# First two column chunks of five stages computed token-major, with the first token tile's part ahead of the second tile's norm

## The reference, cut to what matters

```
h  = norm1(h)                              RMS norm over the 1024 features
cols = h @ w_in                            34 chunks of 256 columns: gates, q, k, v, ...
     recurrence on the first chunks, attention, branches, output product
h  = h + mix
h  = h + (relu(norm2(h) @ w_up) ** 2) @ w_down
```

## Time and profile before

| | us |
|---|---|
| median of 3 runs | 2162.5 (2162.14 to 2163.11) |
| the profiled execution, device time | 2162.1 |
| its span in the trace | 2160.7 |
| PE busy | 2121.8 (98%) |
| DVE busy | 1542.2 (71%) |
| ACT busy | 1337.1 (62%) |
| POOL busy | 42.6 (2%) |
| granted TensorE clock, mean of the run | 0.998 of full |

### The profile page before, as it was taken

The page is one execution under the profiler, slowest core; times in us unless marked ns, Lnnn a source line. Parts: engine busy times, 40 slices in busy tenths (PEclk is TensorE's granted clock), DMA queues, the critical chain, the costliest instruction groups (busy, mean ns, idle before and its releaser), DMA issues.

```text
span 2160.7 us, 31792 instructions
## 1 busy us (share of the span) xinstructions
PE 2121.8 (98%) x13336; PEld 1907.5 (88%) x13336; DVE 1542.2 (71%) x1736; ACT 1337.1 (62%) x1580; POOL 42.6 (2%) x44
## 2 busy tenths in 40 slices
PE   6999999999999999999999899999999999999998
PEld 6899989888888888888888799998998999998986
DVE  5565565699999899989999676666554676666544
ACT  4544436588878887887878474564553654755543
POOL 0000000100000000000000000000110000000100
PEclk9999999999999999999999999999999999999999
DMA  8455554499999999999999555544655465545652
GB/s 280 136 189 186 195 173 144 127 360 361 344 354 371 332 374 349 367 342 358 367 362 372 169 181 167 172 147 142 201 202 192 159 196 170 167 138 158 193 195 78
DMA packets 301591, 511.46 MB, mean 237 GB/s; under 512 B 10496, under 2 KB 177536, under 8 KB 301440
## 3 DMA queue, kind: packets, MB, share of 16 engines
q1 hardware_dynamic: 296464, 498.63, 67.7%
q10 hardware_dynamic: 4976, 10.70, 1.5%
HBM read 503.53 MB, written 1.05 MB: 234 GB/s over the span
## 4 chain that ended last, share of the span: by engine, by line
PE 94%; DVE 5%; issue 1%; ACT 0%; DMA 0%; DVEq 0%; ACTq 0%
PE bank L390 28%; PE bank L392 28%; PE bank L391 28%; PE bank L1756 1%; PE bank L417 1%; PE bank L1352 1%; PE bank L1231 1%; DVE w_low L370 1%; PE bank L423 1%; PE bank L1289 1%; DVE h L553 1%; DVE h L549 1%; DVE stats L542 1%; PE bank L2019 0%; PE bank L1995 0%
## 5 line engine op out<-in xcount | busy, mean ns | idle before, releaser
L370 DVE TENSOR_TENSOR w_low<-raw,w_high 128x1024 fp32r<-128x1024 f32 x938 | 1135.9, 1222 | 420.9 <-ACT w_high L359 405.5
L359 ACT CAST w_high<-raw 128x1024 fp32r<-128x1024 f32 x938 | 979.8, 1052 | 452.4 <-PE bank L392 430.0
L390 PE MATMUL bank<-x,w_high 128*128 128x256 f32 x1712 | 481.6, 281 | 0.0
L391 PE MATMUL bank<-x,w_high 128*128 128x256 f32 x1712 | 477.9, 279 | 0.0
L392 PE MATMUL bank<-x,w_low 128*128 128x256 f32 x1712 | 477.5, 279 | 0.0
L390 PE MATMUL bank<-w_high,x 128*128 128x512 f32 (+1 forms) x976 | 342.9, 351 | 0.0
L392 PE MATMUL bank<-w_high,x 128*128 128x512 f32 (+1 forms) x976 | 338.6, 347 | 0.0
L391 PE MATMUL bank<-w_low,x 128*128 128x512 f32 (+1 forms) x976 | 338.4, 347 | 0.0
L390 PEld LDWEIGHTS bank<-x,w_high 128*128 128x128 f32 x1712 | 321.9, 188 | 0.4
L391 PEld LDWEIGHTS bank<-x,w_high 128*128 128x128 f32 x1712 | 321.9, 188 | 0.2
L392 PEld LDWEIGHTS bank<-x,w_low 128*128 128x128 f32 x1712 | 321.8, 188 | 0.0
(11 more groups left out here) (326 smaller groups left out, 2555.2 us busy)
## 6 DMA issues: line engine op xcount, KB each, us to landing
raw<-in_moe_wd SPq DMA_DIRECT2D x88, 1024.0 KB, 5.5
raw<-in_w_in SPq DMA_DIRECT2D x84, 1024.0 KB, 5.2
raw<-in_moe_wg SPq DMA_DIRECT2D x80, 1024.0 KB, 5.4
raw<-in_moe_wu SPq DMA_DIRECT2D x80, 1024.0 KB, 5.4
raw<-in_w_up SPq DMA_DIRECT2D x32, 1024.0 KB, 5.4
raw<-in_w_down SPq DMA_DIRECT2D x32, 1024.0 KB, 4.9
raw<-in_w_out SPq DMA_DIRECT2D x16, 1024.0 KB, 4.9
raw<-in_ffn_wg SPq DMA_DIRECT2D x11, 1024.0 KB, 5.3
```

The source lines that it names most:

```text
L359: q.copy(high, raw).then_inc(st.cast, 1)
L370: q.tensor_tensor(low, raw, high.bitcast(F32), ALU.subtract).then_inc(st.low_made, 1)
L390: T.matmul(out, stationary[0], moving[0], start=start, stop=False, skip_group_check=True)
L391: T.matmul(out, stationary[0], moving[1], start=False, stop=False, skip_group_check=True)
```

## The change

At five stage entries `tensor_transposes` and `first_product` give way to `tensor_entry`. The first two chunks (four pieces) are now computed token-major: x is stationary, 256 weight columns move, and the output has tokens on partitions. So tile 0's part needs only tile 0's x. After turning tile 0, PE runs its high x high and high x low matmuls, then turns tile 1, then does tile 0's low x high, then tile 1's part whole. The number of product matmuls stays at 96 of 256 columns. Every `used` count of the four pieces comes in the last part. The chunks are then copied (or gated, or squared) as they are, turned to feature-major by four transposes each (`tensor_turned`) after piece 4 (in the feed-forward after pieces 4 and 5, one product of the two chunks), and evicted or split from there.

On ACT and DVE, the copies of tile 0's x stand ahead of tile 1's square and scale, and the addition of tile 1 stands behind tile 0's scale. The casts of the new stage's pieces 1 to 3 stand ahead of these copies. The low halves of pieces 1 to 3 (at layer 0's entry, of piece 3 alone) go from DVE to POOL (`gpsimd_lows`). Matmuls on constants are fewer: 4 and 1 for 8, 2 and 2 in four entries of this kind, 15 and 1 for 26, 1 and 2 at layer 0. The mixers' entries stay.

```diff
+def tensor_entry(k, src, ready, spin_bank, spins, banks):
+    T, st, base = k.nc.tensor, k.weights, 4 * k.transposed
+    first = st.next_piece
+    st.next_piece += 4
+    weights = [st.views(first + i)[1:] for i in range(4)]
+    def part(c, half, t, x_half, w_half):
+        out, w = tile2(k.banks[banks[c]])[:, t, :], weights[2 * c + half][w_half]
+        for kk in range(KT // 2):
+            i = half * (KT // 2) + kk
+            mm = T.matmul(out, k.x[x_half][:, i, t * P:(t + 1) * P], w[:, kk, :],
...
+    tensor_spin(k, spin_bank, spins[0])
+    tensor_turn(k, src, ready, 0)
+    tensor_spin(k, spin_bank, spins[1])
+    for half in range(2):
+        T.wait_ge(k.sem("x_high_made"), base + half + 1)
+        for c in range(2):
+            T.wait_ge(st.cast, first + 2 * c + half + 1)
+            part(c, half, 0, 0, 0)
+    for piece in range(4):
+        if piece == 3:
+            tensor_spin(k, spin_bank, spins[2])
+            tensor_turn(k, src, ready, 1)
+            for half in range(2):
+                T.wait_ge(k.sem("x_made"), base + half + 1)
+                for c in range(2):
+                    part(c, half, 0, 1, 0)
+        T.wait_ge(st.low_made, first + piece + 1)
+        part(*divmod(piece, 2), 0, 0, 1)
+    for c in range(2):
+        for half in range(2):
+            T.wait_ge(k.sem("x_high_made"), base + half + 3)
+            part(c, half, 1, 0, 0)
+            part(c, half, 1, 0, 1)
+        for half in range(2):
+            T.wait_ge(k.sem("x_made"), base + half + 3)
+            part(c, half, 1, 1, 0).then_inc(k.used, 1)
+def gpsimd_lows(k, upto):
+    q, st = k.nc.gpsimd, k.weights
+    while st.next_low <= upto:
+        raw, high, low = st.views(st.next_low)
+        q.wait_ge(st.cast, st.next_low + 1)
+        q.wait_ge(st.low_made, st.next_low)
+        q.tensor_tensor(low, raw, high.bitcast(F32), ALU.subtract).then_inc(st.low_made, 1)
...
 def tensor_layer(k, a, layer):
...
-    for n in range(N_COLS):
+    tensor_entry(k, a.xn, [rms_ready(k, t) for t in range(TT)], 3, (4 if layer else 15, 1, 0), LAYER_ENTRY)
+    for n in range(2, N_COLS):
         for half in range(2):
             tensor_columns(k, layer, n, half)
+            if (n, half) == (2, 0):
+                for c in range(2):
+                    T.wait_ge(k.sem("entered"), 2 * layer + c + 1)
+                    tensor_turned(k, entered(a, c), k.banks[LAYER_TURNED[c]]).then_inc(k.sem("entry_turned"), 1)
...
 def scalar_layer(k, a, layer):
...
-        if p % 2 and p < AT_BRANCH:
+        if p == 4:
+            for c in range(2):
+                scalar_evict(k, a, layer, c)
         scalar_recurrence(k, a, layer, p)
         sides.at(p)
+        if p in (1, 3):
+            scalar_entry(k, a, layer, p // 2)
+        elif p % 2 and p < AT_BRANCH:
             scalar_evict(k, a, layer, p // 2)
...
 def scalar_mlp(k, m, layer):
...
-    for t in range(TT):
-        scalar_rms(k, t, m.xn[:, t, :], norm_source(k, t))
+    scalar_rms(k, 0, m.xn[:, 0, :], norm_source(k, 0))
     scalar_casts(k, k.weights, base + PAIRS - 1)
-    scalar_transposes(k)
+    scalar_transposes(k, (0,))
+    scalar_rms(k, 1, m.xn[:, 1, :], norm_source(k, 1))
+    scalar_transposes(k, (1,))
...
 def vector_mlp(k, m, layer):
...
+    vector_rms(k, 0, m.xn[:, 0, :], *gains)
+    vector_add(k, SUMS, 1, (k.used, base))
+    vector_transposes(k, (0,))
+    vector_rms(k, 1, m.xn[:, 1, :], *gains)
+    vector_transposes(k, (1,))
```

More of the change, by code:

```diff
@@ L461, in tensor_transposes @@
-    ident = k.shared_const("ident")
     for t in range(TT):
         tensor_spin(k, bank, spins[t])
[L464 to L469, removed]
-    tensor_spin(k, 7, spins[TT])
+        tensor_turn(k, src, ready, t)
+    tensor_spin(k, 7, spins[TT])
@@ L551, in vector_layer_norm, with vector_scale @@
     own.up()
+def vector_scale(k, t):
+    V, h, gains = k.nc.vector, k.h, k.gains
+    st, mv, rstd, var = norm_columns(k, t)
     vector_root(k, var, rstd)
@@ L908, in tensor_ffn @@
                     T.wait_ge(k.sem("gate_out" if which == 0 else "gated"), j - 1)
[L909 to L912, removed]
+                mm = product(k, piece, k.x, half, 2 * (j % 2) + which, False)
                 mm.then_inc(k.used, 1)
+            if j == 1 and which == 0:
+                T.wait_ge(k.sem("gated"), 1)
+                tensor_turned(k, m.gate[0], k.banks[4]).then_inc(k.sem("entry_turned"), 1)
     for i in range(FT - TAIL):
@@ L2118, in tensor_columns, with entered, scalar_entry @@
     tokens = n in (VH, VH + 1) or VA <= n < AB
-    mm = product(k, piece, k.x, half, bank_of(n), tokens) if n else first_product(k, piece, half, 0)
-    mm.then_inc(k.used, 1)
+    product(k, piece, k.x, half, bank_of(n), tokens).then_inc(k.used, 1)
+LAYER_ENTRY, LAYER_TURNED = (4, 5), (6, 7)
+def entered(a, c):
+    return a.g[:, 2 * c:2 * c + 2, :]
+def scalar_entry(k, a, layer, c):
+    A_ = k.nc.scalar
+    A_.wait_ge(k.used, AT_LAYER[layer] + 2 * c + 2)
+    A_.copy(entered(a, c), tile2(k.banks[LAYER_ENTRY[c]])).then_inc(k.sem("entered"), 1)
 def tensor_branch(k, src, layer, u, ready):
@@ L2245, in vector_layer @@
     sides = attention_sides(lambda w: vector_attention(k, a, layer, w))
-    for t in range(TT):
-        vector_rms(k, t, a.xn[:, t, :], k.norm1, (k.sem("loaded_norm1"), 16 * (layer + 1)))
-    vector_transposes(k)
+    gains = k.norm1, (k.sem("loaded_norm1"), 16 * (layer + 1))
+    vector_rms(k, 0, a.xn[:, 0, :], *gains)
+    if layer == 0:
+        vector_scale(k, 1)
+    else:
+        vector_add(k, SUMS, 1, (k.used, base))
+    vector_transposes(k, (0,))
+    vector_rms(k, 1, a.xn[:, 1, :], *gains)
+    vector_transposes(k, (1,))
     for p in range(AT_OUT + KT - TAIL):
@@ L2282, in tensor_mlp @@
                 T.wait_ge(k.sem("relu"), 16 * layer + j - 3)
-            mm = product(k, piece, k.x, half, j % 4, False) if j else first_product(k, piece, half, 0)
-            mm.then_inc(k.used, 1)
+            product(k, piece, k.x, half, j % 4, False).then_inc(k.used, 1)
+            if (j, half) == (2, 0):
+                for c in range(2):
+                    T.wait_ge(k.sem("squared_up"), 16 * layer + c + 1)
+                    tensor_turned(k, m.relu[c], k.banks[MLP_TURNED[c]]).then_inc(k.sem("entry_turned"), 1)
     for i in range(NT2 - TAIL):
@@ L2319, in vector_mlp @@
     V, base = k.nc.vector, AT_LAYER[layer] + AT_UP
-    for t in range(TT):
-        vector_rms(k, t, m.xn[:, t, :], k.gains[:, 1, :], (k.sem("loaded_norm2"), 16 * (layer + 1)))
-    vector_transposes(k)
-    vector_lows(k, k.weights, base + PAIRS - 1)
+    gains = k.gains[:, 1, :], (k.sem("loaded_norm2"), 16 * (layer + 1))
+    vector_rms(k, 0, m.xn[:, 0, :], *gains)
+    vector_add(k, SUMS, 1, (k.used, base))
+    vector_transposes(k, (0,))
+    vector_rms(k, 1, m.xn[:, 1, :], *gains)
+    vector_transposes(k, (1,))
     for j in range(NT2 // 2):
@@ L2334, in vector_mlp @@
     vector_add(k, SUMS, 0, (k.sem("half_done"), k.halves))
-    vector_add(k, SUMS, 1, (k.used, base + 2 * NT2))
+    if layer + 1 == DEPTH:
+        vector_add(k, SUMS, 1, (k.used, base + 2 * NT2))
 def gpsimd_mlp(k, m, layer):
```

140 lines of the change are left out of this document (100 added, 40 removed).

## The result

The changed kernel takes 2172.8 us (median of 5, 2171.8 to 2173.2), the kernel before 2162.6 in the same rounds: ratio 1.0046, 95% interval 1.0031 to 1.0060. It is slower by 10 us, where 10 us faster was forecast. Beside the experiments the kernel before took 2161.9 to 2162.0 us, so times of different rounds compare to about 0.6 us. The profiled execution took 2171.8 us, its span is 2170.4, the mean granted clock 0.993 of full.

The account below looks back on a forecast made before the run. PE was taken to bound the kernel (94% of the chain). Gains of 3.5 + 1.7 + 1.9 + 0.9 + 1.9 = 9.9 us off 2162.1 gave 2152.2, with 0.4 for the median 2152.6 us; range 2148.8 to 2158.0.

Parts of the forecast that it names:

- GpSimd's low halves: At the entries: GpSimd's subtractions, 2.38 to 3.16 us each, stay hidden; cost 0, bounds 0 and 1 us in four entries.
- slower: Whole kernel: the outcome of being slower by over 0.2%, given a chance of 0.04.
- the five gains: Feed-forward 3.5 us, layer 0 1.7, its MLP 1.9, layer 1 0.9, its MLP 1.9.
- Tile 1's turning: PE's transposes of tile 1 at the entries: at 119.65 in the feed-forward, 7.0 us into the MLPs.
- What the layers give back: In each layer PE waits for DVE's low halves, 0.7 us at piece 8 and 0.2 at piece 13: 0.9 back.
- Rival 1: At the layers ACT is the new bound, both give all back: 2155.2 us, 2158 with late copies; chance 0.17.
- rival 4: At the entries tile 1's norm is later by as much, only the feed-forward gains: 2159 us; chance 0.06.
- Rival 2: At four entries GpSimd is late, 4 us and more per subtraction, costing 2 us each: 2160 to 2161; chance 0.05.
- Rival 3: At the new entries each of ten pauses drops PE's clock for 5 us: 15 us slower, 2177; chance 0.04.

Follow-up runs that it names:

- e1: Changed kernel with GpSimd's subtractions cut to 2 of 256 columns per row, the rest of those low halves left out: 2151.9 us, ratio 0.9951.
- e7: Changed kernel with each of GpSimd's subtractions cut into eight of 128 columns: 2168.5 us, ratio 1.0030.
- e11: Changed kernel with each of GpSimd's subtractions cut into four of 256 columns: 2158.45 us, ratio 0.9984.
- e10: Changed kernel, GpSimd's low halves starting only after tile 1's scale, PE first taking what needs no new low half, constants refitted: 2156.1 us, ratio 0.9974.
- e8: Kernel before with the root's two small two-tensor instructions written as tensor_scalar with per-partition scalars: 2164.25 us, ratio 1.0011.

## Why the prediction was wrong

**The step that failed** is "GpSimd's low halves", priced at 0 with bounds 0 and 1 us per entry; it cost 20.9 us: 14.4 us in standing instructions of DVE and, through PE's longer pauses, about 5 us of clock. I asked whether the low halves come in time for PE. They did: no row of PE waits for POOL in the kernel after, and three took 8.4 to 8.5 us, within my 7.1 to 9.5. What I never asked was which instructions of DVE start while a subtraction runs. Each root has two that read two SBUF tensors, and the root is what PE waits for.

**How the rows were misread.** The subtraction of 3.16 us in the earlier trace rows began at 414.3, the low half of DVE beside it at 414.07. DVE was first, so GpSimd stood, some 0.8 us of 3.16. From DVE's 1.21 I concluded that the price falls on GpSimd only. The row shows one of two cases; the other, GpSimd first, stands nowhere in the trace before (its 938 low halves on DVE take 1.19 to 1.23 us without exception), and an unseen case should have been bounded by one full subtraction for each of DVE's instructions on two tensors. Two roots by two such instructions by up to 2.4 us in five entries is a bound of tens of us; even a small chance of it would have put slower above 0.04.

The Trainium skill, SBUF — State Buffer, SBUF: two separate sides, says more: the pair of ports that the two engines share is an exclusive lock, taken by a VectorE instruction with two SBUF inputs (against a GpSimd instruction that reads SBUF) or by GpSimd, whichever starts first, for the whole instruction, while the other blocks. The runs agree: a small instruction is held by a whole subtraction (2.33 us) or by an eighth (0.43), and not with one tensor (0.15) or with one operand in PSUM (1.29 for two); where the scale was first, the subtraction took 3.42. I had drawn on the shorter sentence of the Trainium skill, GPSIMD Engine Reference, Specifications, and read a lock as a slowdown.

**The rest, by its own steps.** e1 takes the standing instructions away and lands at 2151.9, against 2152.6 forecast; the table above has the five gains within 0.2 us.
- Tile 1's turning at the feed-forward: forecast 119.65, in e1 119.49. At the MLPs 7.05 us into the entry, in e1 7.08. At layer 0 tile 0 and tile 1 at 10.4 and 16.2, in e1 10.35 and 16.12; at layer 1 tile 1 at 7.15, in e1 7.10.
- What the layers give back: 0.9 in each was forecast, 0.7 of it at piece 8. In after and in e1 PE waits twice for DVE's `w_low`, 1.1 us in sum, so about 0.6 in each layer.
- Rival 1 (ACT bounds the layers) and rival 4 (tile 1's norm is later by as much) did not come.
- Rival 2 (GpSimd late, 2160 to 2161) came only in e7, where I made it so.
- Rival 3, the clock, had the right sign and half the mechanism. Short pauses did not lower it, as I argued: in e1 the entries have six pauses ahead of the turnings, of 0.5 to 1.5 us, and no fall behind them. But pauses of 3.1 to 4.7 us did, in four entries, and those were the work of the failed step. It was worth 5.1 us, not 25. I had also overlooked a row: the trace before has one longer pause, 2.14 us ahead of a turning at 17.90, and its granted clock is 1.00 on both sides.

What stays open is the clock: why it held behind the 3.1 us pause of the last MLP while it fell behind the same pause of the first was not tried. The length of the pause does not settle it alone, for in e11 it fell behind one of 2.44 us (layer 0). About 0.3 us between the spans of after and e1 lie outside the five entries.

## What to carry to other kernels

Before work goes to an idle GpSimd, list what VectorE starts while it runs. Each instruction that reads two SBUF tensors, however small, can wait for the end of the GpSimd instruction; on a chain of small dependent ones it does so several times. Put such work where VectorE reads PSUM or idles, as in e10, or cut it until one part is short, but not so far that it comes late. And when a trace shows two engines side by side, ask which of them was first before saying which pays.

## What was not expected of the hardware

- An instruction on 128x1 elements took 2.33 us in place of 0.22, with no wait for a semaphore in its row: the length of a row can be a wait.
- GpSimd stands too where VectorE is first, but that cost nothing here: 13 subtractions are 35.0 us beside the norms and 31.2 behind them (e10).
- Cutting costs: a subtraction of 1024 columns takes 2.69 us in the mean, four of 256 take 3.64, eight of 128 take 4.43 (waits behind DVE included; by the medians 2.40, 2.94 and 3.65).
- On 128x1, the form with a scalar per partition is slower than the one on two tensors, 273 ns against 220 and 214 against 159, and 20 roots of it show in the time of the kernel (e8).
